# Decode set up inside the projection, new values on GpSimd's queue, output rows stored by the sync queue

## The reference

```python
def diff_attend(q, k, v, mask, lam):
    s = jnp.einsum('bqhmd,bkhmd->bmhqk', q, k).astype(jnp.float32) * (HEAD_DIM ** -0.5)
    if mask is not None:
        s = jnp.where(mask, s, -jnp.inf)
    p = jax.nn.softmax(s, axis=-1)
    a = p[:, 0] - lam * p[:, 1]
    return jnp.einsum('bhqk,bkhe->bqhe', a.astype(v.dtype), v)

def mixer_sublayer(x, conv_prev, k_past, v_past, norm_g, w_in, conv_w, lam, lam_init, head_norm, w_out):
    z = rms_norm(x, norm_g) @ w_in
    b_gate, c_gate, x_in, q, k, v = jnp.split(z, SPLITS, axis=-1)
    ...
        o = diff_attend(q, jnp.concatenate([k_past, k], axis=1),
                        jnp.concatenate([v_past, v], axis=1), None, lam)
```

## Time and profile before

| | us |
|---|---|
| time, median of 3 runs (lowest to highest) | 3612.23 (3609.74 to 3615.14) |
| the profiled execution, its own time | 3616.81 |
| its span, first to last instruction | 3614.5 |
| TensorE busy, share of the span | 3372.7 (93%) |
| VectorE, ScalarE, GpSimd busy | 1689.3, 1286.5, 1033.3 |
| decode, from its first instruction to attend's first | 1255.4 to 1378.7 |
| granted TensorE clock, mean of the span | 0.969 of full speed |

### The profile page before, as it was taken

One profiled execution on the slowest core, in us unless ns is written; L12 is line 12 of the kernel. 1 busy time (PEld: TensorE's weight loads), 2 busy tenths in 40 slices (PEclk: granted clock), 3 DMA queues, 4 the chain that ended last, 5 costly groups with the idle time before them and its releaser, 6 DMA issues. The chain is left out here.

```text
span 3614.5 us, 51248 instructions
## 1 busy us (share of the span) xinstructions
PE 3372.7 (93%) x18439; PEld 2956.0 (82%) x18440; DVE 1689.3 (47%) x1746; ACT 1286.5 (36%) x1573; POOL 1033.3 (29%) x785
## 2 busy tenths in 40 slices
PE   8999999999999887989999959999999999999990
PEld 8999999999999865667888747888888788778770
DVE  4222232001111146871111168558888858846677
ACT  4000000000000034760111147557878757746572
POOL 3444444444444311234445431011111111101010
PEclk9999999999999989999999969999999999999995
DMA  4121111222222392216445369769999969967798
GB/s 149 58 68 54 54 55 58 73 67 75 86 80 60 99 331 81 64 37 233 131 149 160 123 214 362 264 237 361 357 359 363 371 239 376 359 233 258 258 339 359
DMA packets 340570, 691.60 MB, mean 191 GB/s; under 512 B 23034, under 2 KB 150970, under 8 KB 329999
## 3 DMA queue, kind: packets, MB, share of 16 engines
q1 hardware_dynamic: 290228, 585.74, 45.7%
q10 hardware_dynamic: 37163, 66.14, 4.9%
q0 software_dynamic: 13104, 38.69, 3.0%
HBM read 637.25 MB, written 97.28 MB: 203 GB/s over the span
## 5 line engine op out<-in xcount | busy, mean ns | idle before, releaser
L1924 DVE TENSOR_TENSOR e_w_lo<-expert_raw,e_w_hi 128x2048 fp32r<-128x2048 f32 x388 | 873.0, 2289 | 254.7 <-ACT e_w_hi L1836 234.2
L1836 ACT ACTIVATE e_w_hi<-expert_raw 128x2048 fp32r<-128x2048 f32 x388 | 744.4, 1919 | 301.9 <-PE e_gu L1750 252.9
L296 PE MATMUL p_z<-hT_hi,p_w_hi 128*128 128x384 f32 x2256 | 755.0, 335 | 1.6 <-DVE p_xs L416 1.6
L298 PE MATMUL p_z<-hT_hi,p_w_lo 128*128 128x384 f32 x2256 | 753.6, 334 | 0.0
L297 PE MATMUL p_z<-hT_lo,p_w_hi 128*128 128x384 f32 x2256 | 753.6, 334 | 0.0
L296 PEld LDWEIGHTS p_z<-hT_hi,p_w_hi 128*128 128x128 f32 x2256 | 423.5, 188 | 1.9 <-DVE p_xs L416 1.9
L297 PEld LDWEIGHTS p_z<-hT_lo,p_w_hi 128*128 128x128 f32 x2256 | 423.5, 188 | 0.0
L298 PEld LDWEIGHTS p_z<-hT_hi,p_w_lo 128*128 128x128 f32 x2256 | 423.4, 188 | 0.0
L1750 PE MATMUL e_gu<-e_w_hi,e_xT_hi 128*128 128x512 f32 x1216 | 390.2, 392 | 6.5 <-issue 6.4
L1750 PE MATMUL e_gu<-e_w_lo,e_xT_hi 128*128 128x512 f32 x1216 | 387.9, 390 | 0.0
L1750 PE MATMUL e_gu<-e_w_hi,e_xT_lo 128*128 128x512 f32 x1216 | 387.8, 390 | 0.0
(11 more groups left out here) (336 smaller groups left out, 4653.9 us busy)
## 6 DMA issues: line engine op xcount, KB each, us to landing
expert_raw<-w_ei SPq DMA_DIRECT2D x256, 1024.0 KB, 8.5
expert_raw<-w_eo SPq DMA_DIRECT2D x128, 1024.0 KB, 10.3
p_w_raw<-w_in SPq DMA_DIRECT2D x96, 512.0 KB, 3.9
m_w_raw<-w_out SPq DMA_DIRECT2D x64, 512.0 KB, 4.3
d_v<-cache_v SPq DMA_DIRECT2D x8, 2048.0 KB, 8.4
rows_back<-expert_rows SPq DMA_DIRECT2D x12, 1024.0 KB, 15.6
n_x<-x SPq DMA_DIRECT2D x9, 1024.0 KB, 5.1
chunks<-p_e ACTq DMA_DIRECT2D x16, 576.0 KB, 2.8
```

Source lines behind the costliest of these rows:

```text
L296: pe.matmul(out, w_hi[:, k, :], x_hi[:, xk, cols], start=(k == 0), stop=False)
L298: mm = pe.matmul(out, w_lo[:, k, :], x_hi[:, xk, cols], start=False, stop=(k == KT - 1))
L1836: act.activation(w_hi[:, s, :], raw[:, r, :], ACT.Copy).then_inc(hi_done, 1)
L1924: dve.tensor_tensor(w_lo[:, s, :], raw[:, r, :], w_hi[:, s, :], ALU.subtract).then_inc(lo_done[r], 1)
```

## The change

It has five parts.

1. In the turn phase the loads of the norm's rows and of the first half chunk of weights are issued one place earlier. The reciprocal roots are computed ahead of `taps` and lambda; on TensorE the turn of `rstd` comes before the turn of the small rows, and 13 instead of 12 row blocks of products stand ahead of both.
2. Buffers of decode are laid where the first half of `hT` lies, which the projection no longer reads once the last chunk's first half is done (`half0_used`). From that moment SyncE loads queries, new keys, the cached keys of stream 1 and the cached values of stream 0, GpSimd zeroes `d_qx` and `d_vn`, VectorE spreads the queries, TensorE transposes the keys of stream 0, two heads ahead of each of the three blocks of the last half chunk and two behind it, and ScalarE copies all eight heads.
3. The projection no longer waits for its stores. The semaphores and their counts are handed on (`projected`), and in decode GpSimd (ahead of its first load of new values) and SyncE (ahead of the prompt's heads) wait for them.
4. In decode there are three key buffers, the keys of stream b+2 are loaded behind the values of stream b, the key transposes are spread in four pairs over a stream, with another split of the copies between ScalarE and VectorE, and the new values come on GpSimd's queue with a semaphore of their own.
5. Output rows are stored by SyncE, behind the loads of two streams later. Decode doesn't wait for the last of them; in the attention, SyncE (ahead of reading them back) and ScalarE (ahead of its first exponential) do.

```diff
@@ phase_turn
-                load_tile(0)
                 sp.dma_start(g_rows, ...).then_inc(g_loaded, 16)
+                load_tile(0)
+                load(sp, 0, lambda half: w[half, :, :, 2 * DC:2 * DC + P], (0,))
                 load_tile(1)
-                load(sp, 0, lambda half: w[half, :, :, 2 * DC:2 * DC + P], (0,))
...
-                first_products(pe, NB - 1, range(0, 8), z, hT_hi, hT_lo)
-                pe.wait_ge(small_loaded, 16)
...
-                first_products(pe, NB - 1, range(8, 12), z, hT_hi, hT_lo)
+                first_products(pe, NB - 1, range(0, 13), z, hT_hi, hT_lo)
                 pe.wait_ge(rstd_step, 2)
...
+                pe.wait_ge(small_loaded, 16)
...
+                first_products(pe, NB - 1, range(13, KT), z, hT_hi, hT_lo)
@@ phase_project
-                sp.dma_start(first_keys[:], ...).then_inc(keys_loaded, 16)
+                st.load_keys(sp, 0)
+                sp.wait_ge(e_stored, 16 * 2 * CH + 1)
+                sp.wait_ge(half0_used, N + 1)
+                sp.dma_start(st.q[:], ...).then_inc(st.q_loaded, 16)
+                sp.dma_start(st.kn[:], ...).then_inc(st.kn_loaded, 16)
+                st.load_keys(sp, 1)
+                st.load_values(sp, 0)
...
+                pool.wait_ge(half0_used, N + 1)
+                pool.memset(st.qx[:], 0.0).then_inc(st.zeroed, 1)
+                pool.memset(st.vn[:], 0.0).then_inc(st.zeroed, 1)
...
+                for b in range(NB):
+                    st.turn_keys(pe, t_ps, 0, (2 * b, 2 * b + 1), c.ident)
+                    products(pe, N - 1, 1, z, hT_hi, hT_lo, (b,))
+                st.turn_keys(pe, t_ps, 0, (6, 7), c.ident)
                 pe.wait_ge(rows_ready, 2 * CH)
                 turn_back(2 * CH - 1)
...
+                dve.wait_ge(st.zeroed, 1)
+                dve.wait_ge(st.q_loaded, 16)
+                for m in range(2):
...
+                keep_e(2 * CH - 1, 16 * 2 * CH)
                 keep_rows(2 * CH - 1)
...
-                act.wait_ge(tail_stored, 16)
-                act.wait_ge(rows_stored, 16 * 2 * CH + 1)
...
+                for h in range(HEADS):
+                    st.keep_keys(act, t_ps, 0, h)
+                store_rows(io.v_all, CH - 1, 2 * CH - 1)
+    return ((tail_stored, 16), (rows_stored, 16 * 2 * CH + 1), (e_stored, 16 * 2 * CH + 1), ...
@@ phase_decode, SyncE
+                def store_rows(b):
+                    sp.wait_ge(o_kept, G * (b + 1))
+                    for j in range(HG):
+                        sp.dma_start(io.o_new[...], orow[W * j:W * j + NEW, b % 2, :, :]).then_inc(o_stored[b % 2], 16)
+
+                st.load_keys(sp, 2)
+                st.load_values(sp, 1)
+                load_keys(3)
                 for b in range(2, STREAMS):
-                    load_keys(b)
                     load_values(b)
+                    if b + 2 < STREAMS:
+                        load_keys(b + 2)
+                    store_rows(b - 2)
+                for done, count in projected:
+                    sp.wait_ge(done, count)
                 for h in range(2):
                     load_head(c, sp, h, q_heads, k_heads, v_heads, head_loaded)
+                    store_rows(STREAMS - 2 + h)
@@ phase_decode, GpSimd
-                pool.memset(qx[:], 0.0).then_inc(zeroed, 1)
-                pool.memset(vn[:], 0.0).then_inc(zeroed, 1)
-                pool.memset(at[:], 0.0).then_inc(zeroed, 1)
+                pool.memset(at[:], 0.0).then_inc(at_zeroed, 1)
+                for done, count in projected:
+                    pool.wait_ge(done, count)
                 for b in range(STREAMS):
-                    pool.wait_ge(o_kept, G * (b + 1))
-                    for j in range(HG):
-                        pool.dma_start(io.o_new[...], orow[...]).then_inc(o_stored[b % 2], 16)
-                for s in range(2):
-                    pool.wait_ge(o_stored[s], 16 * HG * (STREAMS // 2))
+                    if b >= 2:
+                        pool.wait_ge(o_done, G * (b - 1))
+                    pool.dma_start(vn[0:NEW, b % 2, :], io.v_all[...]).then_inc(vn_loaded[b % 2], 16)
@@ phase_decode, TensorE
-                        pe.wait_ge(v_loaded[b % 2], 32 * (b // 2 + 1))
+                        pe.wait_ge(st.v_loaded[b % st.VB], 16 * (b // st.VB + 1))
+                        pe.wait_ge(vn_loaded[b % 2], 16 * (b // 2 + 1))
...
-                    if b < last:
-                        turn_keys(b + 1, range(0, 4))
+                    turn_keys(b + 1, 0, 1)
                     mix(b, 0)
-                        turn_keys(b + 1, range(4, 6))
+                    turn_keys(b + 1, 2, 3)
                     values(b, 0)
+                    turn_keys(b + 1, 4, 5)
                     mix(b, 1)
-                        turn_keys(b + 1, range(6, 8))
+                    turn_keys(b + 1, 6, 7)
                     values(b, 1)
@@ phase_attend
             def _(sp):
+                for done, count in streams_stored:
+                    sp.wait_ge(done, count)
                 sp.dma_start(so[:], io.o_new...).then_inc(so_loaded, 16)
...
                 act.wait_ge(hn_kept, 1)
+                for done, count in streams_stored:
+                    act.wait_ge(done, count)
```

More of the change, by code:

```diff
@@ L254, in _ @@
                     mm.then_inc(rstd_turned, 1)
-                first_products(pe, NB - 1, range(12, KT), z, hT_hi, hT_lo)
+                pe.wait_ge(small_loaded, 16)
+                for j in range(CH):
+                    mm = pe.transpose(tp[:, 3, j * 19:(j + 1) * 19], small[:, j * P:(j + 1) * P], c.ident[0:19, 0:19])
+                mm.then_inc(small_turned, 1)
+                first_products(pe, NB - 1, range(13, KT), z, hT_hi, hT_lo)
 def weight_chunks(c, tag, w_raw, w_hi, w_lo):
@@ L284, in split_half, with products @@
         pool.tensor_tensor(w_lo[:, part, :], w_raw[:, part, :], w_hi[:, part, :], ALU.subtract).then_inc(split[half], 1)
-    def products(pe, n, half, z, x_hi, x_lo):
+    def products(pe, n, half, z, x_hi, x_lo, blocks=range(NB)):
         pe.wait_ge(split[half], n + 2)
-        for b in range(NB):
+        for b in blocks:
             if half == 0:
@@ L338, in phase_project @@
         tp = mem.enter_context(nc.psum_tensor("p_tp", [P, NB, 512], F32))
-        load, split_half, products, _, z_done, z_kept, _ = chunks_of_weights
+        t_ps = mem.enter_context(nc.psum_tensor("p_t", [P, 2, 512], F32))
+        load, split_half, products, _, z_done, z_kept, half0_used, _ = chunks_of_weights
         zeroed, step = sem("p_zeroed"), sem("p_conv_step")
@@ L395, in _ @@
                 pe.wait_ge(tail_kept, 1)
-                with pe.Fori(1, 2 * CH) as m:
+                with pe.Fori(1, 2 * CH - 1) as m:
                     products(pe, m + NQ, 0, z, hT_hi, hT_lo)
@@ L400, in _ @@
                     products(pe, m + NQ, 1, z, hT_hi, hT_lo)
+                products(pe, N - 1, 0, z, hT_hi, hT_lo)
+                pe.wait_ge(rows_ready, 2 * CH - 1)
+                turn_back(2 * CH - 2)
+                for b in range(NB):
+                    st.turn_keys(pe, t_ps, 0, (2 * b, 2 * b + 1), c.ident)
+                    products(pe, N - 1, 1, z, hT_hi, hT_lo, (b,))
+                st.turn_keys(pe, t_ps, 0, (6, 7), c.ident)
                 pe.wait_ge(rows_ready, 2 * CH)
@@ L733, in _ @@
                 dve.wait_ge(mixer_step, 2)
-                dve.wait_ge(zeroed, 3)
-                dve.wait_ge(q_loaded, 16)
-                for m in range(2):
-                    part = slice(m * DH, (m + 1) * DH)
-                    dve.tensor_copy(qx[part, :, :, m * NEW:(m + 1) * NEW],
-                                    qs[part, :, :].rearrange("p h (b q) -> p b h q", b=STREAMS)).then_inc(qx_ready, 1)
-                keep_keys(0, range(1, HEADS, 2))
+                dve.wait_ge(at_zeroed, 1)
                 for b in range(STREAMS):
@@ L756, in _ @@
             def _(act):
-                def keep_keys(b, heads):
-                    for h in heads:
-                        act.wait_ge(k_turned, b * HEADS + h + 1)
-                        act.activation(kT[:, b % 2, h, :], t_ps[:, 0, :], ACT.Copy).then_inc(kT_ready[0], 1)
                 def exps(b, hg):
@@ L773, in keep_rows, with keep_keys @@
                     act.activation(orow[:, b % 2, hg, :], o_ps[:, 0:VD], ACT.Copy).then_inc(o_kept, 1)
-                keep_keys(0, range(0, HEADS, 2))
+                def keep_keys(b, *heads):
+                    if b < STREAMS:
+                        for h in heads:
+                            st.keep_keys(act, t_ps, b, h)
                 for b in range(STREAMS):
@@ L778, in _ @@
                     exps(b, 1)
-                    if b < last:
-                        keep_keys(b + 1, (0, 2, 4))
+                    keep_keys(b + 1, 0, 2)
                     keep_rows(b, 0)
-                    if b < last:
-                        keep_keys(b + 1, (6,))
+                    keep_keys(b + 1, 4, 6)
                     keep_rows(b, 1)
```

(1 more changed line is left out.)

164 lines of the change are left out of this document (88 added, 76 removed).

## The result

| | us |
|---|---|
| before, median of 5 runs | 3611.46 (3609.41 to 3615.14) |
| after, median of 5 runs | 3590.53 (3588.38 to 3594.16) |
| ratio, with its 95% interval | 0.9946 (0.9936 to 0.9957) |
| the profiled execution after: span, its own time | 3588.5, 3590.53 |

The account below looks back on a forecast made before the run. Decode was taken as bound neither by one engine nor by transfers alone, but by waits. Gains of 0.8 (turn phase), 15.8 (to decode's end) and 4.2 (end) sum to 20.8 us: median 3591.4, range 3580 to 3603.

Parts of the forecast that it names:

- Turn phase, 0.8: Turn phase: TensorE's 1.20 us wait for the roots goes, VectorE's lambda chain is late next; gain 0.8 us, bounds 0.3 and 1.4.
- Tail, -2.8: Projection's last half chunk: key transposes among the products delay the issue of the last store by 2.8 us.
- The store, 9.8 us to its landing: Seam to decode: the last store shares engines piece for piece with decode's loads, landing at 1264.1 instead of 1257.7 undisturbed.
- The wait at the first values, 8.9: Stream 0 of decode: TensorE stands 8.9 us until the store and then the new values (5.4 us) have landed.
- The other reading: New values on GpSimd's queue: VectorE, holding the shared port, would cause the 5.4 us; without it the result is 3.7 lower.
- Clock behind the wait, 4.4: Stream 0, behind the wait at the first values: a low clock loses 4.4 us, bounds 0 and 4.4.
- Streams, 11.13: Decode: six streams take 11.13 us each, without waits for keys and with the mixing matrix late next.
- Last stream, 0: Decode's last stream: 10.0 us to its last rows, as in the kernel before; no gain.
- The end, 4.2: Last rows to attention: 6.7 us become 2.5, four store issues and the engines' meeting; gain 4.2, bounds 3 and 4.6.
- From the profile to the median: Whole kernel: the profiled execution lay 4.6 us above the median, so forecast 3596.0 became a median of 3591.4.
- The rival "the store isn't stretched": Seam: the store lands at 1257.7, TensorE stands 2.5 us; gain 27.2, time 3585.0; chance 0.25.
- The slower rival: Decode: row stores behind loads on SyncE's queue hold ScalarE in six streams; 23.0 us slower, 3635.2; chance 0.06.

Follow-up runs that it names:

- two pairs of profiles: The kernel before and the changed kernel as first profiled, and each run once more without edit; the repeats had medians of 3610.21 and 3591.52 us.
- loads_behind: Changed kernel with the keys of stream 1 and values of stream 0 loaded only once the store before the last has landed; 3589.84 us, ratio 0.9938.
- phase_waits: Changed kernel with ScalarE waiting again at the projection's end until all its stores have landed; 3589.62 us, ratio 0.9949.
- loads_ahead: Changed kernel with decode's first two loads (keys of stream 2, values of stream 1) issued in the projection, ahead of the last store; 3601.44 us, ratio 0.9976.
- vn_first: Changed kernel with the first new values moved from GpSimd's queue to SyncE's, ahead of decode's loads; 3590.16 us, ratio 0.9939.
- rows_on_pool: Changed kernel with the output rows stored on GpSimd's queue again, decode still not waiting for the last of them; 3593.74 us, ratio 0.9952.
- the second profile: The kernel before, run and profiled once more without edit; 3610.21 us, ratio 1.0005.

## Why the prediction was right, and where it wasn't

The sum of 20.8 us came out, by the table above as 25.2 and 17.6 in two pairs of profiles and 18.6 to 20.9 in the medians. Step by step:

- **Turn phase, 0.8: wrong.** It is 0 to 0.3. The forecast named VectorE's lambda chain as late next. What was late next is VectorE's first work of the projection, one step further on, whose wait grew by the 0.8 us that the roots had given.
- **Tail, -2.8: right.** -3.0 and -3.1. A wait of VectorE for the store before the last (1.91 instead of 0.83 us) came behind it and held decode's start back by about 1 us, as loads_behind shows. I had not looked at the other store beside which SyncE's early loads run.
- **The store, 9.8 us to its landing: wrong, 3.9.** The step that failed is the start of the loads' bytes, taken as 1.1 us after their issue from an idle moment. Here, with the store flowing, the first pieces came 2.4 us after the issue, when 1111 of the store's 1152 pieces had gone; in phase_waits, with nothing flowing, the same load began after 1.0 to 1.1. By the forecast's own sign, a store that lands in under 5 us, this step was wrong. What stood behind that step is right: loads_ahead shows the store stretched to 18.7 us, and the store before the last shows 547 to 538 pieces, 4 KB beside 512 bytes, like the earlier trace rows (whose 166 small packets are 300 bytes each in the mean, 0.05 MB in all, and not 144, which changes nothing in the count). The rule of the Trainium skill (DMA: Bandwidth & Descriptors, "SWDGE vs HWDGE vs iDMA"), by which the store would have landed 1 us late, seems to fit 3.9 against 3.4 us, but for another reason; where queues do share, the pieces went one for one whatever their size.
- **The wait at the first values, 8.9: wrong with it, 2.90 and 2.71.** Of the 6.0 us that the first one lacks, 4.9 are the new values, which landed at 1264.6 and not at 1269.5, and 1.1 are TensorE's own work ahead of them: it got there at 1261.84 and not at 1260.7, as its clock was 0.79 in that stretch, a cost that the sum had at nothing. From the store's landing on the sum had 5.4 us for the new values; it was 0.6 to GpSimd's issue and 6.4 from there. Full queues make them: 2.0 us first in SyncE's queue (vn_first), 2.5 on GpSimd's with empty DMA engines (loads_ahead). The other reading, from the Trainium skill (SBUF — State Buffer, "Who interferes with whom"), has VectorE hold up such a load. In phase_waits the load took 7.1 us although VectorE stood idle for 1.5 us right behind its issue, so a long landing doesn't need VectorE, and no run here shows VectorE holding one.
- **Clock behind the wait, 4.4: too much.** From the first values to the second stream are 7.0 us instead of 9.9; the clock was back at 1.00 by 1268.
- **Streams, 11.13: right.** 10.97, as VectorE's mixing matrix ends only a wait of 0.2 us. Both causes hold, each by its own experiment: the spread of the transposes 5.5 us, keys two streams ahead 5.1 in the profile and about 7 in the medians.
- **Last stream, 0: wrong, -2.7.** The clock fell there, as in seven of the twelve profiles of the changed kernel and its variants, which nothing before showed.
- **The end, 4.2: nearly right, 3.5, for another reason.** What went is mostly the stand behind GpSimd's last issue, 2.7 us by rows_on_pool, and only 0.8 is the wait for the stores' landing. The two new waits in the attention cost nothing, as forecast.
- **From the profile to the median: wrong.** I took off the 4.6 us by which the profiled execution lay above the median, as if the changed kernel had them too. But against the second profile that execution lost 6.0 us in the streams, to the clock behind waits that the change removes, and 1.7 in a turn phase whose clock changes from execution to execution; and the profiled execution after lay at its median. Without this step the forecast would have been 3596.0.

So the number was right because errors cancelled: by the first pair of profiles the start of the attention was forecast about 4.5 us too late (6.3 at the seam, 1.8 in the turn phase, the tail and the six streams, less 2.8 for the clock in the last stream and 0.7 at the end), and then 4.6 us were taken off that the changed kernel didn't have. The rival "the store isn't stretched" had the right moments, but for a reason that loads_ahead refutes. The slower rival, row stores that hold ScalarE, stayed away only by a margin: in vn_first, loads that start 3.2 us later behind the first scores, under streams that come 4.5 us earlier, were enough. One thing stays open: the setup inside the projection, the largest part at the seam, was not taken back by itself. Its worth is read from the table only, 9.3 us from the last turn to the second stream less 3.0 for the transposes.

## What to carry to other kernels

A transfer can only stretch another if its bytes come in time: work out when both flow, with the start of a load taken from a moment that is like the one in question. Before a profile's distance from the median is taken off a forecast, take a second profile of the same kernel and find the stage in which it lies; where the clock falls behind a wait in one execution and not in the next, the stage's time is a range. When a wait is handed on to a later place, ask whether the same landing ends the next wait; here it did, and only moving other work in front of it gained.

## What the runs showed of the hardware that I had not expected

- A load issued while another queue's store was flowing showed its first pieces 2.4 us after its issue; with idle DMA engines it took 1.0 to 1.1 us (phase_waits). The other way round, a store issued while loads flowed had its first piece after some 3.7 us (loads_ahead), where an idle moment took about 1 us.
- Once both flow, the queues go one for one whatever the size of their pieces: 891 packets of a store in 512-byte pieces beside 897 of loads in 4 KB pieces in loads_ahead, 538 beside 547 in the changed kernel.
- A phase whose last work on GpSimd is the issue of transfers ended 3.59 us after that issue; behind SyncE's four stores (1350.41 + 2.46) the attention began 0.7 us later.
- The issue of four row stores on SyncE's queue took 2.46 to 3.46 us in the changed kernel and 8.85 us in vn_first, where four loads of 2 MB ahead of them in the same queue had not landed when the issue began; in the changed kernel there were at most three.
- The granted clock behind one and the same wait of 2.95 us for keys was 0.50 over six microseconds in one execution and 0.85 in the next.
